# Small-block matmuls of the gate and up projections taken four weight rows at a time, with raw weight rows held in the ring

## The reference, cut to what matters

```
g = minimum(xb @ w_gate[e] + b_gate[e], 7.0)
u = clip(xb @ w_up[e] + b_up[e], -7.0, 7.0)
act = g * sigmoid(1.702 * g) * (u + 1)
y = (act @ w_down[e] + b_down[e]) * gate[:, None]
```

## Time and profile before

| | |
|---|---|
| median of 3 runs | 2564.62 us (2563.2 to 2566.47) |
| the profiled execution's own time | 2563.0 us |
| its span, first to last instruction | 2561.0 us |
| TensorE busy | 2383.3 us, 93% of the span |
| VectorE, ScalarE, GpSimd busy | 57%, 41%, 36% |
| DMA | 505.32 MB, mean 197 GB/s |
| mean granted TensorE clock | 0.966 of full speed |

### The profile page before, as it was taken

The page is one execution under the profiler, slowest core; times in us unless marked ns, Lnnn a source line. Parts: engine busy times, 40 slices in busy tenths (PEclk is TensorE's granted clock), DMA queues, the critical chain, the costliest instruction groups (busy, mean ns, idle before and its releaser), DMA issues.

```text
span 2561.0 us, 34876 instructions
## 1 busy us (share of the span) xinstructions
PE 2383.3 (93%) x11094; PEld 1523.4 (59%) x11095; DVE 1452.3 (57%) x1855; ACT 1039.8 (41%) x1053; POOL 911.7 (36%) x514
## 2 busy tenths in 40 slices
PE   5997999999999996489999999999999999999996
PEld 3443444446666554367766666666667666666774
DVE  3210333342111124378887777778788778777885
ACT  1111122231111000266666465556556565555663
POOL 2220111100000000547654453555556545544763
PEclk8998999999999997689999999999999999999998
DMA  4114101000111221489998888889889888788995
GB/s 149 66 41 100 41 25 32 26 25 25 50 50 58 91 98 64 173 286 347 340 319 285 270 292 289 277 295 314 290 298 314 292 298 288 266 312 278 326 339 166
DMA packets 180116, 505.32 MB, mean 197 GB/s; under 512 B 18082, under 2 KB 60578, under 8 KB 180066
## 3 DMA queue, kind: packets, MB, share of 16 engines
q1 hardware_dynamic: 163874, 457.97, 50.4%
q0 software_dynamic: 16192, 46.67, 8.2%
HBM read 468.34 MB, written 32.05 MB: 195 GB/s over the span
## 4 chain that ended last, share of the span: by engine, by line
PE 78%; DVE 8%; issue 6%; DMA 2%; ACT 2%; DVEq 1%; POOL 1%; SPq 1%; ACTq 0%; POOLq 0%; PEldq 0%
PE psum L1403 12%; PE psum L1405 11%; PE psum L1404 11%; PE psum L1217 6%; PE psum L1272 6%; PE psum L1306 4%; PE psum L1414 4%; PE psum L1350 4%; DVE w_lo L1072 3%; PE psum L1318 2%; PE psum L1317 2%; PE psum L1316 2%; PE psum L1449 2%; PE psum L1256 2%; PE psum L1244 1%
## 5 line engine op out<-in xcount | busy, mean ns | idle before, releaser
L1072 DVE TENSOR_TENSOR w_lo<-ring,w_hi 128x2048 fp32r<-128x2048 f32 x384 | 874.8, 2308 | 84.2 <-ACT w_hi L707 70.5
L707 ACT ACTIVATE w_hi<-ring 128x2048 fp32r<-128x2048 f32 x384 | 721.2, 1918 | 178.6 <-DMA ring<-in_w_down 91.8
L551 POOL TENSOR_SCALAR pick<-iota_bf,slot_col 128x256 bf16<-128x256 bf16 x272 | 513.5, 1900 | 62.5 <-DVE slot_col L1088 62.4
L1403 PE MATMUL psum<-w_hi,xT_hi 128*128 128x512 f32 x1024 | 424.1, 414 | 36.6 <-DVE w_lo L1072 31.1
L1405 PE MATMUL psum<-w_hi,xT_lo 128*128 128x512 f32 x1024 | 407.3, 398 | 0.0
L1404 PE MATMUL psum<-w_lo,xT_hi 128*128 128x512 f32 x1024 | 406.9, 397 | 0.0
L557 POOL DMA_INDIRECT xg<-h_rows,idx_new x33 | 83.8, 2539 | 586.1 <-issue 540.0
L1403 PEld LDWEIGHTS psum<-w_hi,xT_hi 128*128 128x128 f32 x1024 | 193.7, 189 | 157.5 <-issue 65.1
L1405 PEld LDWEIGHTS psum<-w_hi,xT_lo 128*128 128x128 f32 x1024 | 193.8, 189 | 47.0
L1404 PEld LDWEIGHTS psum<-w_lo,xT_hi 128*128 128x128 f32 x1024 | 194.4, 190 | 39.9
L1403 PE MATMUL psum<-w_hi,aT_hi 128*128 128x512 f32 x512 | 214.4, 419 | 3.3 <-DVE aT_lo L1112 3.3
(11 more groups left out here) (237 smaller groups left out, 3032.1 us busy)
## 6 DMA issues: line engine op xcount, KB each, us to landing
ring<-in_w_gate SPq DMA_DIRECT2D x256, 512.0 KB, 5.5
ring<-in_w_up SPq DMA_DIRECT2D x256, 512.0 KB, 6.6
ring<-in_w_down SPq DMA_DIRECT2D x256, 512.0 KB, 4.7
ring<-in_w_in SPq DMA_DIRECT2D x28, 512.0 KB, 4.6
ring<-in_x SPq DMA_DIRECT2D x16, 512.0 KB, 4.1
ring<-in_w_in SPq DMA_DIRECT2D x6, 1024.0 KB, 7.9
vb<-oT SPq DMA_DIRECT2D x16, 256.0 KB, 6.6
ring<-in_w_o SPq DMA_DIRECT2D x4, 1024.0 KB, 6.0
```

Of the source, the lines that this page charges most:

```text
L551: e.tensor_scalar(pick[:, t, :], iota_bf[:, :], slot_col[:, t, :], None, ALU.is_equal).then_inc(g_pick, 1)
L707: e.activation(w_hi[:, hs, :], ring[:, slot, :], ACT.Copy).then_inc(g_hi, 1)
L1072: e.tensor_tensor(w_lo[:, hs, :], ring[:, slot, :], w_hi[:, hs, :].bitcast(F32), ALU.subtract).then_inc(g_lo, 1)
L1403: e.matmul(dst, hi, w_up, start=start, stop=False)
```

## The change

It does the small block's gate/up matmuls in two groups of 32 instructions in place of four groups of 16: behind the wait of k = 3 for k = 0 to 3, and behind that of k = 7 for k = 4 to 7. The raw rows of these chunks stay in the ring until then, so that `room` now waits for later chunks. It does so in all passes, since `room` does not look at the flags.

```
-PAIRED = (2, 8, 10, 12)
+HELD = {2: 1, 8: 3, 9: 2, 10: 1, 12: 3, 13: 2}
...
             def room(p, c0):
 
                 c = c0 - NSLOT
-                hold(e, g_chunk, 12 * p + (c + 1 + (c in PAIRED)))
+                hold(e, g_chunk, 12 * p + (c + 1 + HELD.get(c, 0)))
...
             def extra_of(k, b):
 
-                return (k - 1, k) if b and k % 2 else ()
+                return tuple(range(k - 3, k + 1)) if b and k % 4 == 3 else ()
```

## The result

| | before | after |
|---|---|---|
| median | 2564.62 us | 2777.36 us (2768.55 to 2778.73, 5 runs) |
| ratio after / before | | 1.0817, 95% interval 1.08 to 1.0835 |
| span of the profiled execution | 2561.0 us | 2776.0 us |
| mean granted TensorE clock | 0.966 | 0.946 |

The account below looks back on a forecast made before the run. TensorE was taken to set the time in the passes. The profiled 2563 us plus 152 of waits net of merges plus 13 for the clock gave 2728, against the median 2730 us; eight-in-ten range 2660 to 2815.

Parts of the forecast that it names:

- the likeliest case: Waits at chunks 14, 10, 18 and 8, clock mostly held: 2730 us, 2700 to 2765; chance 0.48.
- Chunk 14: Its load waits for chunk 11, not 9: data need 9.7 us, TensorE 6.6, so 3.1 us of waiting in every iteration.
- Chunk 18 and the next 8: Where down has no small block: 1.9 us of waiting at 18 (30 in all), 1.2 more at 8 (18 in all).
- Chunk 10: Gate/up with a small block: 1.1 us of waiting, 0.8 net of that merge's saving, in 15 passes.
- The merge's saving: Four small-block groups become two in gate/up: 2 x 0.3 us of entry and exit saved in 15 passes, 9 us.
- The clock: TensorE's clock falls to half at six of 31 gaps, 2.2 us each: 13 us; bounds 0 and 87.
- rival (3): The clock falls at all or nearly all gaps of chunk 14, costing 68 us: 2785 us; chance 0.24.
- the one at 863 us: A gap of 2.14 us behind dense products, where the clock held; the four of 2.93 or 2.94 followed small matmuls.
- Rival (2): Only chunk 14 waits in full and chunk 18 is hidden: 2669 us; chance 0.14.
- Rival (4): Loads stay as slow as chunk 14's before the change, 8.2 us, adding 102 us: 2819 us; chance 0.08.
- Rival (5): The loads are hidden and only the merges count, saving 9 us: 2556 us; chance 0.04.
- Rival (6): Both signs cancel, or the load is not delayed: no change in time; chance 0.02.

Follow-up runs that it names:

- e1: The kernel before with the change's late loads but without its merges, small-block groups left in pairs; 2728.3 us, 1.0642 of the kernel before.
- e2: The kernel before with groups of 32 behind k = 3 and 7, loads early, rows of k - 1 and k taken twice; 2584.1 us, ratio 1.0083.
- e8: The kernel before with only the second half merged, 32 instructions behind k = 7 taking rows of 6 and 7 twice, loads early; 2565.9 us, ratio 1.0007.
- e5: The changed kernel with 22 extra bf16 matmuls (2.3 us) between chunks 13 and 14; 2750.9 us, 1.0723 of the kernel before.
- e7: Against the kernel before: groups (0, 1), (2 to 5), (6, 7), load of 16 two chunks later only with a small block; 2605.6 us, ratio 1.0163.

## Why the prediction was right, and where it was off

The kernel got slower, as said, and the time is in the range of eight in ten; 2730 was said and 2777 came, above the 2765 at which the likeliest case ended. In the profiled execution the stretch from the first to the last biases grew by 210.9 us: gaps +147.2, clock +68.8, rest -5.1. Another 3.6 us came behind it.

- **Chunk 14: right.** 3.1 us were predicted for each of 31 iterations; the gaps are 95.7/31 = 3.09 us. The chain of 9.7 us (issue, landing, rounding, rest) was read from four rows and measured as 1271.60 - 1261.57 = 10.0 in the iteration shown. The assumption that the landing would be fast again held: 4.7 us behind the second issue, 5.1 behind the first, in place of the 8.2 of before. For the lower bound, a landing in 4.4 us, no run gives a case: the fastest landing of chunk 14 in any of them took 4.74 (e1).
- **Chunk 18 and the next 8: right in mechanism, 18 smaller.** 30 us were said for 18, 21.4 came (15 waits of 1.43); 18 us more at chunk 8, 17.5 came (32.4 - 14.9). Where down has a small block it was hidden, as said.
- **Chunk 10: right that it waits, smaller.** 1.1 us in 15 passes were said, 16.5 us; the gaps grew by 9.8. In e2, where nothing else delays TensorE, they grew by 17.6.
- **The merge's saving: its size right, its worth wrong.** Entry and exit cost 0.3 us: from the last product ahead of a group to the second behind it are 2.513 us for 16 instructions and 4.240 for 32 (medians), and 2 x 2.513 - 4.240 - 0.47 = 0.32 us per merge, 9.5 us over 30. The prediction took this as a gain on the path. Only 5 us were left in the change and 3 in e2. Chunks that are now late pay 0.26 us of re-entry each; in e8 that closes the sum, and for the change and e2 it was not added up chunk by chunk.
- **Waits and saving together.** The 152 us of the sum are net of the 9 us saved: 161 us of waiting were said and 147.2 came, and net of what the rest fell it is 142.1. So this part of the sum was 10 us too high, which by luck made up for some of the clock's miss. An iteration without small blocks took 48.2 us where 46.6 were said, one with both 58.1 where 55 were said.
- **The clock is the step that failed:** "I take six of 31 at 2.2 us, 13 us". 25 of 31 gaps at chunk 14 had the clock fall, and so had 9 gaps of 1.35 to 1.85 us at chunks 8 and 10: 68.8 us by the rows where 13 were said. The two iterations stand at 0.93 and 0.94, under the 0.95 that the prediction had named as the sign of rival (3). The four gaps before the passes were the better guide, and the one at 863 us the exception. Of the 68.8 us in the rows, e5 bears on the 57 at chunk 14: about 35 of them reach the end.
- **Rival (3)**, 2785 us with the clock falling nearly always, came nearer than the forecast. Its sum of 68 us agrees with the rows. The rule of the Trainium skill, "TensorE: Matmul & The Clock Gate", "HAM oscillation — how this bites in real kernels", that each such wait for data sends the clock back to half, held for 25 of 31 gaps at chunk 14. The clock also fell at nine gaps under 2 us in this kernel, shorter waits than those that the section describes.
- **Rival (2)** is out: 18 waited in 15 of the 16 iterations in which it could. **Rival (4)** is out by the landings. **Rival (5)** is out: the loads are not hidden. Even with early loads the two merges lose 0.8% (e2), and the second alone gains nothing (e8). **Rival (6)** is out: the time changed by 8.2%.

The trace of before had a fifth case, which the prediction left out: a gap of 2.11 us behind the dense products and the biases at the start of the loop. The clock was at half from 1095.1 on, before the next gap began:

```profile
1091.39 0.39 PE L1405 MATMUL psum<-w_hi,xT_lo 128*128 128x512 f32 x1
1091.72 1.03 PE L1428 MATMUL psum<-brow_gu,ones_bf 3*128 3x512 bf16 x4
1094.86 1.56 PE L1396 MATMUL psum<-ident,xg 128*128 128x128 f32 x7 [2.11 <-DVE ut L1097]
```

```profile
1092.70:1094.90 2.20, 0.09 (x2) 0.07 (x2) 2.01 (x2) 0.00 (x0) 0.00 (x0) 1.00 1.02 417
1095.00:1108.00 13.00, 7.13 (x37) 6.02 (x37) 8.86 (x15) 12.99 (x12) 4.23 (x2) 0.50 0.43 151
```

What stays open: why the clock falls at some gaps of 1.5 to 1.9 us and not at others of the same length (8 of the 26 gaps of this length in the changed kernel had a fall, and one of 1.35 us had; in the kernel before, from 1109 us to the last biases, there were two gaps over 1.6 us and no fall). e5 shows that the gap at chunk 14 brings the fall; it does not show how long a gap has to be.

## What to carry to other kernels

Before a buffer is held longer, write down two times from the event that will now release it: what the reader still has to do from there, and the whole chain of the refill, from issue over landing to each engine that prepares the data. Here 6.6 stood against 9.7 us, and the 3.1 us between them came true in each of 31 iterations; the share of DMA time that is free did not tell of it: the passes with small blocks, with a share of 0.81, waited 3.0 us at chunk 14 and the others, with 0.99, 3.2. A short group of work ahead of a chunk may be the cover of that chunk's preparation: moving it saves its entry and exit and pays them back as a wait and a re-entry. Count a gap of TensorE of three microseconds as a gap and a loss of clock: it was both in 25 of 31 here, and by e5's estimate the clock added about 35 us to 93 us of gaps.

## What the runs showed of the hardware

- TensorE's clock fell to half at 25 of 31 gaps of 2.7 to 3.4 us between dense products, inside the gap or up to 1.4 us behind it, and the stretches at half were 3.4 or 6.8 us long, some of them partly in the gap. It also fell at nine gaps of 1.35 to 1.85 us, and four times in e7 where the only gap over 0.15 us in the 4.5 us before was 0.6 to 0.7 us. Each of these four gaps stood behind the matmuls of the biases, which use 3 rows of the array (`3*128`).
- A product that had to wait for a semaphore starts a sequence about 0.26 us dearer than one whose semaphore had long been set (medians at chunks 10 and 14 of e2), beside the idle time that the gap column shows; about 0.16 of it is that the column counts from the end of the product before. A chunk behind another in a dense sequence, with its data long there, costs 0.00.
- A load of 1 MB from an idle queue is steady: issue to last landing of chunk 14 was 4.83 to 5.35 us in 31 iterations of the changed kernel (median 4.97), with the DMA engines at a share of 0.00 to 0.02 in the microsecond ahead of the issue; before, amid other traffic, 5.00 to 8.73 (median 7.39), with a share of 0.7 or more in 30 of the 31.
